# Inside the last unit of a hybrid decoder block: a later scan, output weights' low parts on both sides of it, and row 1's addition moved into the convolution

## The chip, the cores and the metric

The kernel runs on one core of one Trainium2 chip. The metric is the device time of one execution in microseconds (us); lower is better. A core has five engines that run their own instruction lists and meet only at semaphores: TensorE (PE in the rows: matrix products), VectorE (DVE), ScalarE (ACT), GpSimd (POOL), and SyncE (SP, whose queue issues all of this kernel's DMAs).

## The reference, cut to what matters

One decoder layer on x of 2048 positions by 1024 channels, float32:

```python
h = rmsnorm(x, norm_mix); proj = h @ w_in            # 4 groups of 512 channels: x_lru, g_lru, v_cm, g_cm
c = causal_depthwise_conv(x_lru, conv4_w) + conv4_b  # width 4
r, i = sigmoid(c @ gate_a + b_a), sigmoid(c @ gate_x + b_x)   # block diagonal
a = exp(-8 r softplus(-lambda));  b = sqrt(1 - a*a) * i * c
h_t = a_t * h_{t-1} + b_t                            # the scan over positions
y_lru = h * gelu(g_lru)
d = causal_depthwise_conv(v_cm * sigmoid(g_cm), dw31_w) + dw31_b   # width 31
y_cm = silu(layernorm(d))
x = x + concat(rmsnorm(y_lru), rmsnorm(y_cm)) @ w_out
x = x + (silu(rmsnorm(x) @ w_gate) * (rmsnorm(x) @ w_up)) @ w_down
out = rmsnorm(x)
```

## The kernel before, in words

Every large product is made of three float32r products: each operand is split into a high part (a cast by ACT) and a low part (operand minus high part, by POOL or DVE), and PE multiplies high by high, low by high and high by low (lines 1828 to 1830).

**Units.** The part up to the scan is done in 8 units (`UNITS`), one for each of 4 groups of 128 channels and 2 halves of 1024 positions. Unit u has two projections on PE, the short convolution, the gates, the scan of unit u (`scan(u)`, DVE) and the convolution of width 31 (`conv31(u)`, DVE): 31 instructions ("taps") on 128x1024, one after the other, each adding to `acc`. `conv31` is also the timetable of DVE: a table of places (tap numbers) says ahead of which tap other work is put. `scan(u - 1)` stands inside `conv31(u)`; the scan of the last unit, `scan(7)`, comes behind the last convolution.

**The last unit, u = 7.** PE has finished the projections and goes on as far as it may with what follows. Inside `conv31(7)` DVE also does:
- `w_out_lo(n)`, n = 0 to 3: the low parts of two chunks of the output weights each, 2 instructions. ACT makes the high parts ahead of it (`w_out_hi(n)`, line 1186). Pairs 0 and 1 lie in the two buffers `w_raw`; SP may load pair 2 only when `w_out_lo(0)` is done, and pair 3 when `w_out_lo(1)` is done (lines 466 to 469, semaphore `s_wlo`), and both loads stand in SP's queue behind the store of unit 6's y, which waits for POOL's product of the scan's result (`output(6)`, line 726).
- `norm_centre(1)`: tile 1 of 512 positions minus its mean. ACT squares the result (`squares_cm(1)`), POOL folds the squares' four chunks into one (`fold(1, "var")`, lines 789 and 791), PE makes the variance (`norm_var(1, 6)`).
- `add_row(w)` for w = 0: row tile w is 128 positions. PE multiplies y by the output weights into 4 banks of PSUM, two column halves for each of the two head groups; `add_row(w)` scales each bank by the group's rms and adds it to the residual, 4 instructions, each of which waits for its bank (`s_out[e]`). PE may write a bank again for row w + 1 only when `add_row(w)` has read it (`s_outf[e]`).

Behind `conv31(7)` DVE does `scan(7)`, `norm_scale(1)`, and for each row w: `add_row(w)` (for w > 0), a reciprocal, and `hn`, the normalised row for the FFN (line 1656).

PE's order there: gates of unit 7, `norm_mean(1)`, the products of row 0, `norm_sums_lru(1)`, `norm_var(1)`, the products of row 1, the turning of row 0's `hn` by 8 transposes (`turn_h2(0)`, line 1984), the products of row 2, `turn_h2(1)`, and so on through 16 rows. PE waits in order: what stands first holds what is behind it.

ACT's order there: `w_out_hi(0)`, `w_out_hi(1)`, the sigmoids of the gates of unit 7 (which wait for `scan(6)`, since they overwrite `uw`), `y_split(0)` (high part of row 0's y), `gate_functions(7)` (tanh, exp, one minus), and so on to `root(7)`. POOL's order: `output(6)`, the gated input, low part of y of row 0 (`y_lo`, line 820), `decay(7)` (line 757), `decay_square(7)` (line 762), `y_lo` of row 1, `scan_input(7)` (line 781), `fold(1, "var")`, `y_lo` of row 2.

After the 16 rows come the FFN's products (Strassen-like, with halves and sums) and the down projection; PE is their clock.

Of the kernel before, what the change touches and what calls it, by code (L numbers as in the profile page):

```python
# [30 lines left out]
def hybrid_block(nc, x, norm_mix, w_in, conv4_w, conv4_b, gate_a_w, gate_a_b, gate_x_w, gate_x_b,  # L31
# [14 lines left out]
    UNITS = NH * NJ  # L46
# [30 lines left out]
    with ExitStack() as ctx:  # L77
# [260 lines left out]


        SCAN_AT, CENTRE_AT, LATE_AT = 22, 16, 27  # L340
        W_OUT_AT = (12, 14, 17, 19)
        CENTRE_AT_LAST, ROW0_AT = 16, 24
        X_NORM_AT = (7, 8, 9, 10, 12, 13, 14, 15)
        X_LO_AT = (9, 10, 11, 12, 14, 15, 16, 17)
        SCAN_AT_LAST = 11
        NORM_STEP = {2: 2, 3: 5}

        TURN_FIRST = {(1, 0, 0): 0, (1, 0, 4): 1, (1, 1, 0): 2, (1, 1, 4): 3}
# [35 lines left out]
        def yb(w):  # L384

            return w % 2 + 2 * (w // TPH)
# [3 lines left out]
        def w_out_gain(k):  # L390

            return col(k % NJ, R_ONL if k < NJ else R_ONC)
# [560 lines left out]
        def _(act):  # L953
# [3 lines left out]
            def step(ins):  # L957

                steps[0] += 1
                ins.then_inc(s_act, 1)  # L960
                act.wait_ge(s_act, steps[0])
# [23 lines left out]
            def squares_lru(m):  # L985
                act.wait_ge(s_nld[m], 32)
                a.activation(ny[m][:, :, :], ny[m][:, :, :], ACT.Square).then_inc(s_sqy, 1)
# [98 lines left out]
            def gate_functions(u):  # L1086

                j = u % NJ
                act.wait_ge(s_rr, NS * (u + 1))
                if u == 0:  # L1090
                    act.wait_ge(s_rate, 3)
                a.activation(su[:, :], uw[:, :], ACT.Tanh, scale=rate[:, j:j + 1]).then_inc(s_te, 1)
                step(a.activation(uw[:, :], uw[:, :], ACT.Exp, scale=rate2[:, j:j + 1]))
                a.activation(uw[:, :], uw[:, :], ACT.Identity, bias=1.0).then_inc(s_te, 1)

            def two_minus(u):

                act.wait_ge(s_p, u + 1)
                a.activation(su[:, :], uw[:, :], ACT.Identity, scale=-1.0, bias=two[:, 0:1]).then_inc(s_two, 1)
# [79 lines left out]
            def w_out_hi(n):  # L1179

                q = PPAIRS + n
                act.wait_ge(s_w[q % 2], 32 * (q // 2 + 1))
                if n == 0:
                    act.wait_ge(s_pair[3], PPAIRS)
                for e in range(2):
                    ins = a.activation(wo_hi[:, 2 * n + e], w_raw[q % 2][:, e].rearrange("p k c -> p (k c)"),
                                       ACT.Copy, scale=w_out_gain(2 * n + e))
                ins.then_inc(s_whi, 1)

            def y_split(w):  # L1190
                act.wait_ge(s_yl[w % 2], 32 * (w // 2 + 1))
                if w >= 2:
                    act.wait_ge(s_out[3], w - 1)
                a.copy(y_hi[yb(w)][:, :, :], y_raw[yb(w)][:, :, :]).then_inc(s_yhi, 1)
# [4 lines left out]
            gates(UNITS - 1)  # L1199
            act.wait_ge(s_fin, UNITS - 1)  # L1200
            y_split(0)
            gate_functions(UNITS - 1)
            w_out_hi(2)
            two_minus(UNITS - 1)
            w_out_hi(3)
            squares_lru(1)
            y_split(1)
            squares_cm(1)
            root(UNITS - 1)
            y_split(2)  # L1210
# [210 lines left out]
        def _(dve):  # L1421
# [73 lines left out]
            def norm_centre(m, bank):  # L1495

                dve.wait_ge(s_mean, m + 1)
                v.tensor_tensor(nd[m][:, :, :], nd[m][:, :, :], ps[bank][:, None, :].broadcast_to([P, NJ, TILE]),
                                ALU.subtract).then_inc(s_dc, 1)
# [39 lines left out]
            def add_row(w, between=None):  # L1539

                if w == 4:
                    norm_rms(1)
                if w % 4 == 0:
                    dve.wait_ge(s_rms, w // 4 + 1)
                dve.wait_ge(s_xr[w % 4], 16 * (w // 4 + 1))
                line = row[w % 4]
                for group in range(2):
                    if group and between:
                        between()
                    for dh in range(2):  # L1550
                        e = 2 * group + dh
                        cols = slice(dh * TILE, (dh + 1) * TILE)
                        dve.wait_ge(s_out[e], w + 1)
                        if group:
                            dve.wait_ge(s_outf[dh], w + 1)
                        v.scalar_tensor_tensor(out=line[:, cols], in0=ps[e],
                                               scalar=rms[:, 2 * w + group:2 * w + group + 1],
                                               in1=line[:, cols], op0=ALU.mult, op1=ALU.add).then_inc(s_outf[e], 1)

            def conv31(u):  # L1560
                j = u % NJ
                t = glu[u % 2]
                last = 0
                for k in range(TAPS31):
                    place = k
                    if u == NJ - 1:

                        for g in range(TPH):
                            if place == X_NORM_AT[g]:
                                x_norm(TPH + g)  # L1570
                            if place == X_LO_AT[g]:
                                x_lo(TPH + g)
                    if place == CENTRE_AT and u == N0:
                        norm_centre(0, 6)
                    if u >= 1 and place == (SCAN_AT_LAST if u == UNITS - 1 else SCAN_AT):
                        scan(u - 1)
                    if u == UNITS - 1 and place == ROW0_AT:
                        norm_rms(0)
                        add_row(0)
                    if u == UNITS - 1 and place == CENTRE_AT_LAST:  # L1580
                        norm_centre(1, 6)
                    if u == UNITS - 1 and place in W_OUT_AT:
                        w_out_lo(W_OUT_AT.index(place))
                    if place == LATE_AT:
                        if u == N0 + 1:
                            norm_scale(0)
                    if k == 0:
                        dve.wait_ge(s_glu, (NS + 1) * (u + 1))
                        if u >= 1:
                            dve.wait_ge(s_conv31, u)  # L1590
                        ins = v.tensor_scalar(acc[:, :], t[:, 0:HALF], col(j, R_DW), col(j, R_DWB), ALU.mult, ALU.add)
                    else:
                        dve.wait_ge(s_dve, last)
                        if k == TAPS31 - 1 and u >= 2:
                            dve.wait_ge(s_dst[u % 2], 16 * (u // 2))
                        into = dst[u % 2] if k == TAPS31 - 1 else acc
                        ins = v.scalar_tensor_tensor(out=into[:, :], in0=t[:, k:k + HALF], scalar=col(j, R_DW + k),  # L1597
                                                     in1=acc[:, :], op0=ALU.mult, op1=ALU.add)
                    if k == TAPS31 - 1:
                        ins.then_inc(s_conv31, 1)  # L1600
                    else:
                        steps[0] += 1
                        last = steps[0]
                        ins.then_inc(s_dve, 1)
# [35 lines left out]
                    weight_sum(0, 0, n, 1)  # L1640

            for w in range(NT):
                if w:
                    add_row(w, first_weight_sums if w == NT - 1 else None)
                if w == 0:
                    norm_scale(1)
                if w == NT - 1:
                    a_low(0, 2)
                dve.wait_ge(s_std2, w + 1)
                step(v.reciprocal(rstd[:, w:w + 1], rstd[:, w:w + 1]))  # L1650
                if w == 0:
                    dve.wait_ge(s_gmix, 32)
                    dve.wait_ge(s_rm1, 1)
                if w >= 2:
                    dve.wait_ge(s_tr[1], w - 1)
                v.scalar_tensor_tensor(out=hn[w % 2][:, :], in0=row[w % 4][:, :], scalar=rstd[:, w:w + 1],
                                       in1=g_row[:, :], op0=ALU.mult, op1=ALU.mult).then_inc(s_hn, 1)
                for m, first in NORM_STEP.items():
                    if w - first == 0:
                        norm_centre(m, 4)  # L1660
                    if w - first == 2:
                        norm_scale(m)
                    if w - first == 4:
                        norm_rms(m)
                if w in SUM_AT:
                    for n in range(2):
                        first_half_sum(2 * SUM_AT.index(w) + n)
# [489 lines left out]
```

## Time and profile before

| | us |
|---|---|
| three timed executions | 2006.25, 2002.8, 2006.49 (median 2006.25) |
| the profiled execution, its own time | 2004.53 |
| its span in the trace | 2002.7 |
| PE busy | 1893.2 (95%) |
| POOL busy | 1249.3 (62%) |
| DVE busy | 1125.7 (56%) |
| ACT busy | 816.8 (41%) |

The span is the time from the first to the last instruction in the trace. PE is the busiest engine by far, but in the two slices of the page from 400 to 500 us, around the last unit, it is busy for seven and eight tenths, and so DVE comes level with it there (eight tenths in both).

### The profile page before, as it was taken

Reading aid. Unit: us, or ns where it says so; the run is one execution under the profiler, and the core shown is the slowest. Engines: PE = TensorE matmul, PEld = TensorE weight load, DVE = VectorE, ACT = ScalarE, POOL = GpSimd, SP = SyncE. Lnnn points to the kernel's source line nnn. Section 1 sums busy time; section 2 is a strip of 40 time slices with the busy share of each in tenths; the row PEclk is TensorE's granted clock in tenths of the full one; section 3 lists DMA queues with packets and bytes.
Section 4 is the critical chain, followed back from the end, with each engine's and each line's share of the span. In section 5 each row is a group of like instructions: output and inputs, shape, how many; then the busy total and the mean of one; then the engine's idle time right before and its main releaser. Section 6 shows DMA issues by size and latency. Waiting matters only on the chain.

```text
span 2002.7 us, 22412 instructions
## 1 busy us (share of the span) xinstructions
PE 1893.2 (95%) x8338; PEld 1554.0 (78%) x8338; DVE 1125.7 (56%) x1023; ACT 816.8 (41%) x936; POOL 1249.3 (62%) x490
## 2 busy tenths in 40 slices
PE   6999899978999799999999789999999899999997
PEld 5888687756888678878878668888888688888886
DVE  5899899988554635454454644444453123434446
ACT  6356856585553523333233433233333222322234
POOL 2477477964542567887666556766766666766663
PEclk9999999988999899999999989999999999999999
DMA  5223232245768334445234622233233565565555
GB/s 165 64 60 98 74 95 74 77 144 182 241 207 280 101 100 131 140 136 152 84 100 129 219 87 86 93 115 101 89 112 134 220 248 205 175 217 180 180 189 209
DMA packets 242335, 284.97 MB, mean 142 GB/s; under 512 B 12078, under 2 KB 167726, under 8 KB 241754
## 3 DMA queue, kind: packets, MB, share of 16 engines
q1 hardware_dynamic: 242266, 284.04, 42.9%
q8 instruction: 45, 0.74, 0.2%
q14 instruction: 24, 0.20, 0.0%
HBM read 201.68 MB, written 82.31 MB: 142 GB/s over the span
## 4 chain that ended last, share of the span: by engine, by line
PE 69%; POOL 12%; issue 7%; DVE 5%; DMA 3%; ACT 2%; SPq 1%; POOLq 0%; DVEq 0%; ACTq 0%
PE ps L1828 17%; PE ps L1829 17%; PE ps L1830 17%; PE acc L1828 6%; PE acc L1829 5%; PE acc L1830 5%; POOL b_lo L826 2%; POOL t_lo L832 2%; POOL gt L872 1%; POOL quad L881 1%; DVE acc L1597 1%; POOL fs L890 1%; DMA y_raw<-d_scr 1%; POOL f_lo L917 1%; DMA wd_raw<-in_w_down 1%
## 5 line engine op out<-in xcount | busy, mean ns | idle before, releaser
L1597 DVE SCALAR_TENSOR_TENSOR acc<-glu,par,acc 128x1024 f32<-128x1024 f32 x232 | 298.9, 1288 | 7.2
L832 POOL TENSOR_TENSOR t_lo<-t_sum,t_hi 128x2048 fp32r<-128x2048 f32 x44 | 205.0, 4658 | 135.2 <-ACT t_hi L1241 135.2
L826 POOL TENSOR_TENSOR b_lo<-m_raw,b_hi 128x1536 fp32r<-128x1536 f32 x44 | 163.9, 3724 | 164.5 <-ACT b_hi L1236 164.5
L917 POOL TENSOR_TENSOR f_lo<-f_raw,f_hi 128x2048 fp32r<-128x2048 f32 (+1 forms) x42 | 180.9, 4306 | 133.2 <-ACT f_hi L1381 133.2
L1636 DVE TENSOR_TENSOR t_sum<-m_raw 128x512 f32<-128x512 f32 x88 | 131.1, 1491 | 214.0 <-PE ps L1830 97.1
L1828 PE MATMUL ps<-h_hi,w_hi 128*128 128x512 f32 x512 | 201.9, 394 | 4.6 <-POOL w_lo L720 2.7
L1829 PE MATMUL ps<-h_lo,w_hi 128*128 128x512 f32 x512 | 200.0, 391 | 0.0
L1830 PE MATMUL ps<-h_hi,w_lo 128*128 128x512 f32 x512 | 200.0, 391 | 0.0
L1828 PE MATMUL ps<-wd_hi,f_hi 128*128 128x512 f32 x462 | 181.4, 393 | 9.9 <-POOL wd_lo L924 9.9
L1381 ACT CAST f_hi<-f_raw 128x2048 fp32r<-128x2048 f32 (+1 forms) x42 | 74.2, 1768 | 274.6 <-PE ps L1830 178.2
L1829 PE MATMUL ps<-wd_lo,f_hi 128*128 128x512 f32 x462 | 181.0, 392 | 0.0
L1830 PE MATMUL ps<-wd_hi,f_lo 128*128 128x512 f32 x462 | 180.8, 391 | 0.0
L1828 PE MATMUL ps<-a_hi,t_hi 128*128 128x512 f32 x440 | 171.4, 390 | 1.5 <-DVE p5s L1694 0.8
L1829 PE MATMUL ps<-a_lo,t_hi 128*128 128x512 f32 x440 | 171.2, 389 | 0.0
L1830 PE MATMUL ps<-a_hi,t_lo 128*128 128x512 f32 x440 | 171.2, 389 | 0.0
L1779 DVE TENSOR_TENSOR wd_raw<-wd_raw 128x1024 f32<-128x1024 f32 (+1 forms) x30 | 71.7, 2390 | 171.6 <-DMA wd_raw<-in_w_down 171.6
L1828 PE MATMUL acc<-a_hi,t_hi 128*128 128x512 f32 x264 | 106.6, 404 | 26.5 <-DVE a_lo L1612 17.0
L1828 PE MATMUL ps<-wo_hi,y_hi 128*128 128x512 f32 x256 | 107.6, 420 | 18.6 <-DVE wo_lo L1534 11.2
L1828 PEld LDWEIGHTS ps<-h_hi,w_hi 128*128 128x128 f32 x512 | 96.6, 189 | 25.2 <-POOL w_lo L720 3.2
L1636 DVE TENSOR_TENSOR t_sum<-m_raw,t_sum 128x512 f32<-128x512 f32 x88 | 112.6, 1280 | 3.0
L1830 PEld LDWEIGHTS ps<-h_hi,w_lo 128*128 128x128 f32 x512 | 96.5, 189 | 20.5
L1829 PEld LDWEIGHTS ps<-h_lo,w_hi 128*128 128x128 f32 x512 | 96.6, 189 | 19.6 <-issue 0.2
(212 smaller groups left out, 4603.0 us busy)
## 6 DMA issues: line engine op xcount, KB each, us to landing
f_raw<-f_scr SPq DMA_DIRECT2D x35, 1024.0 KB, 5.0
wd_raw<-in_w_down SPq DMA_DIRECT2D x60, 512.0 KB, 6.6
f_scr<-fs SPq DMA_DIRECT2D x110, 256.0 KB, 2.0
m_raw<-in_w_gate SPq DMA_DIRECT2D x88, 256.0 KB, 4.0
m_raw<-in_w_up SPq DMA_DIRECT2D x88, 256.0 KB, 5.0
w_raw<-in_w_in SPq DMA_DIRECT2D x32, 512.0 KB, 5.3
f_scr<-gt SPq DMA_DIRECT2D x44, 256.0 KB, 2.0
xt<-in_x SPq DMA_DIRECT2D x16, 512.0 KB, 3.7
```

The costliest lines, as they stand in the source:

```text
L826: g.tensor_tensor(b_lo[b][:, :, :, :], m_raw[b][:, 0:3], f32(b_hi[b][:, :, :, :]), ALU.subtract).then_inc(s_mlo, 1)
L832: g.tensor_tensor(t_lo[b][:, :, :, :], t_sum[b][:, :, :, :], f32(t_hi[b][:, :, :, :]), ALU.subtract).then_inc(s_mlo, 1)
L872: g.tensor_tensor(tile, tile, source[:, :], ALU.mult).then_inc(s_fm, 1)
L881: g.tensor_tensor(quad[:, into], quad[:, x1], quad[:, x2_], op).then_inc(s_qs, 1)
L917: g.tensor_tensor(f_lo[j % 3][:, 0:n], f_raw[j % 2][:, 0:n], f32(f_hi[j % 3][:, 0:n]), ALU.subtract).then_inc(s_dlo, 1)
L1381: a.copy(f_hi[j % 3][:, 0:n], f_raw[j % 2][:, 0:n]).then_inc(s_dhi, 1)
L1597: ins = v.scalar_tensor_tensor(out=into[:, :], in0=t[:, k:k + HALF], scalar=col(j, R_DW + k), in1=acc[:, :], op0=ALU.mult, op1=ALU.add)
L1636: v.tensor_tensor(into, in0, in1, ALU.subtract).then_inc(s_t, 1)
L1779: v.tensor_tensor(raw[:, 0, 0:c1 - c0], raw[:, 0, 0:c1 - c0], raw[:, 1, 0:c1 - c0], WD[m][2]).then_inc(s_t, 1)
L1828: pe.matmul(bank, lhs[0](c), rhs[0](c), start=first, stop=False, skip_group_check=more)
L1829: pe.matmul(bank, lhs[0](c), rhs[1](c), start=False, stop=False, skip_group_check=more)
L1830: mm = pe.matmul(bank, lhs[1](c), rhs[0](c), start=False, stop=last, skip_group_check=more)
```

## The change

In the last unit alone, DVE's timetable, ACT's order and the place of one addition change. `scan(6)` goes from tap 11 to tap 17; the four `w_out_lo` from taps 12, 14, 17, 19 to 16, 17, 20, 21; `norm_centre(1)` from 16 to 23; `add_row(0)` from 24 to 25; `add_row(1)`, which stood behind the convolution, gets place 29. Where places agree, the scan comes ahead of `w_out_lo`. ACT does `w_out_hi(2)` and `w_out_hi(3)` ahead of `gate_functions(7)`, and `y_split(1)` ahead of `two_minus(7)`. No instruction is added or taken away; POOL, SP and PE keep their order.

```diff
@@ -338,11 +338,11 @@
         SCAN_AT, CENTRE_AT, LATE_AT = 22, 16, 27
-        W_OUT_AT = (12, 14, 17, 19)
-        CENTRE_AT_LAST, ROW0_AT = 16, 24
+        W_OUT_AT = (16, 17, 20, 21)
+        CENTRE_AT_LAST, ROW0_AT, ROW1_AT = 23, 25, 29
...
-        SCAN_AT_LAST = 11
+        SCAN_AT_LAST = 17
@@ -1199,12 +1199,12 @@
             gates(UNITS - 1)
             act.wait_ge(s_fin, UNITS - 1)
             y_split(0)
+            w_out_hi(2)
+            w_out_hi(3)
             gate_functions(UNITS - 1)
-            w_out_hi(2)
+            y_split(1)
             two_minus(UNITS - 1)
-            w_out_hi(3)
             squares_lru(1)
-            y_split(1)
             squares_cm(1)
             root(UNITS - 1)
@@ -1579,6 +1579,8 @@
                         norm_centre(1, 6)
+                    if u == UNITS - 1 and place == ROW1_AT:
+                        add_row(1)
                     if u == UNITS - 1 and place in W_OUT_AT:
@@ -1640,7 +1642,7 @@
             for w in range(NT):
-                if w:
+                if w >= 2:
                     add_row(w, first_weight_sums if w == NT - 1 else None)
```

DVE in the last unit around the scan and the output weights, before (L1523 is the scan, L1534 `w_out_lo`, L1597 the taps, L1498 `norm_centre(1)`):

```order
L1597 SCALAR_TENSOR_TENSOR acc<-glu_168,par,acc 128x1024 x10
L1523 SCALAR_TENSOR_TENSOR cv_132<-uw,hl,su 128x1024
L1597 SCALAR_TENSOR_TENSOR acc<-glu_168,par,acc 128x1024
L1534 SCALAR_TENSOR_TENSOR wo_lo<-w_raw_140,par,wo_hi 128x1024 x2
L1597 SCALAR_TENSOR_TENSOR acc<-glu_168,par,acc 128x1024 x2
L1534 SCALAR_TENSOR_TENSOR wo_lo<-w_raw_141,par,wo_hi 128x1024 x2
L1597 SCALAR_TENSOR_TENSOR acc<-glu_168,par,acc 128x1024 x2
L1498 TENSOR_TENSOR nd_174<-nd_174,ps 128x2048
```

The same place of DVE's list with the change (two lines were added, so the taps are L1599):

```order
L1599 SCALAR_TENSOR_TENSOR acc<-glu_168,par,acc 128x1024 x15
L1534 SCALAR_TENSOR_TENSOR wo_lo<-w_raw_140,par,wo_hi 128x1024 x2
L1599 SCALAR_TENSOR_TENSOR acc<-glu_168,par,acc 128x1024
L1523 SCALAR_TENSOR_TENSOR cv_132<-uw,hl,su 128x1024
L1534 SCALAR_TENSOR_TENSOR wo_lo<-w_raw_141,par,wo_hi 128x1024 x2
L1599 SCALAR_TENSOR_TENSOR acc<-glu_168,par,acc 128x1024 x3
L1534 SCALAR_TENSOR_TENSOR wo_lo<-w_raw_140,par,wo_hi 128x1024 x2
L1599 SCALAR_TENSOR_TENSOR acc<-glu_168,par,acc 128x1024
L1534 SCALAR_TENSOR_TENSOR wo_lo<-w_raw_141,par,wo_hi 128x1024 x2
L1599 SCALAR_TENSOR_TENSOR acc<-glu_168,par,acc 128x1024 x2
L1498 TENSOR_TENSOR nd_174<-nd_174,ps 128x2048
```

Five more taps and a pair of output weights now stand ahead of the scan, and `norm_centre(1)` stands behind all four pairs.

The end of the last convolution on DVE and what follows it, before (L1556 is `add_row`, L1504 and L1506 `norm_scale(1)`, L1650 and L1656 the reciprocal and `hn`):

```order
L1556 SCALAR_TENSOR_TENSOR row_169<-ps,rms,row_169 128x512 x4
L1597 SCALAR_TENSOR_TENSOR acc<-glu_168,par,acc 128x1024 x6
L1597 SCALAR_TENSOR_TENSOR dst_149<-glu_168,par,acc 128x1024
L1523 SCALAR_TENSOR_TENSOR cv_133<-uw,hl,su 128x1024
L1504 RECIPROCAL nrs_178<-nrs_178 128x512
L1506 TENSOR_TENSOR nd_174<-nd_174,nrs_178 128x2048
L1650 RECIPROCAL rstd<-rstd 128x1
L1656 SCALAR_TENSOR_TENSOR hn_190<-row_169,rstd,g_row 128x1024
L1556 SCALAR_TENSOR_TENSOR row_170<-ps,rms,row_170 128x512 x4
```

And with the change:

```order
L1556 SCALAR_TENSOR_TENSOR row_169<-ps,rms,row_169 128x512 x4
L1599 SCALAR_TENSOR_TENSOR acc<-glu_168,par,acc 128x1024 x4
L1556 SCALAR_TENSOR_TENSOR row_170<-ps,rms,row_170 128x512 x4
L1599 SCALAR_TENSOR_TENSOR acc<-glu_168,par,acc 128x1024
L1599 SCALAR_TENSOR_TENSOR dst_149<-glu_168,par,acc 128x1024
L1523 SCALAR_TENSOR_TENSOR cv_133<-uw,hl,su 128x1024
L1504 RECIPROCAL nrs_178<-nrs_178 128x512
L1506 TENSOR_TENSOR nd_174<-nd_174,nrs_178 128x2048
L1652 RECIPROCAL rstd<-rstd 128x1
L1658 SCALAR_TENSOR_TENSOR hn_190<-row_169,rstd,g_row 128x1024
```

The four additions of row 1 (`row_170`) stood behind row 0's `hn`; now two taps, the scan, `norm_scale(1)` and row 0's `hn` stand behind them.

ACT's list from row 0's high part on (L1186 is `w_out_hi`, L1092 to L1094 `gate_functions(7)`, L1099 `two_minus(7)`, L1194 `y_split`, L987 and L991 the two squares), as a difference:

```order
 L1194 CAST y_hi_154<-y_raw_150 128x1024
-L1092 ACTIVATE su<-uw,rate 128x1024
-L1093 ACT_TABLE_LOAD
-L1093 ACTIVATE uw<-uw,rate_197 128x1024
-L1094 ACTIVATE uw<-uw 128x1024
 L1186 ACTIVATE wo_hi<-w_raw_140,par 128x1024 x2
-L1099 ACTIVATE su<-uw,two 128x1024
 L1186 ACTIVATE wo_hi<-w_raw_141,par 128x1024 x2
+L1092 ACTIVATE su<-uw,rate 128x1024
+L1093 ACT_TABLE_LOAD
+L1093 ACTIVATE uw<-uw,rate_197 128x1024
+L1094 ACTIVATE uw<-uw 128x1024
```

The gate functions now stand behind the scaling of pairs 2 and 3, which wait for their loads.

## Rows read from the trace of the kernel before

**Rows 1.** Busy times by stretch: window, its us, then each engine's busy us, PEclk.

```profile
400.00:500.00 100.00, 77.72 (x325) 61.57 (x323) 86.87 (x63) 67.14 (x74) 53.30 (x24) 0.83 0.47 162
500.00:650.00 150.00, 150.00 (x721) 123.86 (x720) 78.68 (x86) 69.26 (x100) 63.61 (x28) 1.00 0.77 242
```

**Rows 2.** Chain that ended last, 430 to 496 us: start, us, what.

```profile
432.98 4.43 DVE cv L1523
...
438.59 3.52 DVE wo_lo L1534 x2
...
493.54 0.23 PE ps L1828
```

**Rows 3.** PE in order of time: start, us, operation, [idle before <- releaser].

```profile
450.20 0.77 PE L1828 MATMUL ps<-wo_hi,y_hi 128*128 128x512 f32 x1 [3.91 <-DVE wo_lo L1534]
...
464.72 0.80 PE L1828 MATMUL ps<-wo_hi,y_hi 128*128 128x512 f32 x1 [7.33 <-DVE wo_lo L1534]
...
470.42 0.39 PE L1829 MATMUL ps<-wo_lo,y_hi 128*128 128x512 f32 x1
...
476.42 1.29 PE L1879 MATMUL ps<-nsq,mean_w 128*128 128x512 f32 x2
...
489.67 0.39 PE L1830 MATMUL ps<-wo_hi,y_lo 128*128 128x512 f32 x1
492.45 1.09 PE L1984 MATMUL ps<-ident,hn 128*128 128x128 f32 x8 [2.39 <-DVE hn L1656]
```

**Rows 4.** DVE in order of time, last unit.

```profile
412.36 13.21 DVE L1597 SCALAR_TENSOR_TENSOR acc<-glu,par,acc 128x1024 f32<-128x1024 f32 x10
432.98 4.43 DVE L1523 TENSOR_TENSOR_SCAN cv<-uw,hl,su 128x1024 f32<-128x1024 f32 x1 [7.40 <-POOL su L781]
...
452.49 2.28 DVE L1498 TENSOR_TENSOR nd<-nd,ps 128x2048 f32<-128x2048 f32 x1
...
455.88 2.47 DVE L1534 SCALAR_TENSOR_TENSOR wo_lo<-w_raw,par,wo_hi 128x1024 fp32r<-128x1024 f32 x2
...
471.30 2.73 DVE L1556 SCALAR_TENSOR_TENSOR row<-ps,rms,row 128x512 f32<-128x512 f32 x4
...
483.08 2.35 DVE L1523 TENSOR_TENSOR_SCAN cv<-uw,hl,su 128x1024 f32<-128x1024 f32 x1
...
491.11 1.28 DVE L1656 SCALAR_TENSOR_TENSOR hn<-row,rstd,g_row 128x1024 f32<-128x1024 f32 x1
```

**Rows 5.** ACT in order of time, last unit.

```profile
431.78 4.26 ACT L1186 ACTIVATE wo_hi<-w_raw,par 128x1024 fp32r<-128x1024 f32 x4
437.49 1.28 ACT L1080 ACT_TABLE_LOAD   x1 [1.45 <-DVE cv L1523]
...
444.07 1.15 ACT L1092 ACTIVATE su<-uw,rate 128x1024 f32<-128x1024 f32 x1
...
448.67 2.18 ACT L1186 ACTIVATE wo_hi<-w_raw,par 128x1024 fp32r<-128x1024 f32 x2
452.32 1.15 ACT L1099 ACTIVATE su<-uw,two 128x1024 f32<-128x1024 f32 x1 [1.47 <-POOL uw L757]
...
459.86 1.91 ACT L991 ACTIVATE nsq<-nd 128x2048 f32<-128x2048 f32 x1
...
463.08 1.06 ACT L1104 ACTIVATE su<-su 128x1024 f32<-128x1024 f32 x1
```

**Rows 6.** POOL in order of time, last unit.

```profile
432.91 2.35 POOL L810 TENSOR_TENSOR c_lo<-cv,c_hi 128x1024 fp32r<-128x1024 f32 x1
...
464.21 2.69 POOL L781 TENSOR_TENSOR su<-su,cv 128x1024 f32<-128x1024 f32 x1 [1.82 <-ACT su L1104]
...
469.31 1.28 POOL L791 TENSOR_TENSOR nsq<-nsq 128x512 f32<-128x512 f32 x1
```

**Rows 7.** DMA issues, 430 to 470 us: operation, KB each, median us to landing.

```profile
w_raw<-in_w_out SPq DMA_DIRECT2D x4, 512.0 KB, 3.9
```

**Rows 8.** SP's queue in order of time: start, us of issuing, which DMA.

```profile
442.14 8.75 SPq L468 DMA_DIRECT2D w_raw<-in_w_out  x4
```

## The prediction

> **What bounds the kernel now.** I read four views. The busy times by stretch come first: from 400 to 500 us PE is busy for 77.7 of 100 us at a mean granted clock of 0.83 of full, and from 500 to 650 us for 150.0 of 150 [rows 1]. So PE bounds the kernel on both sides of the last unit, and inside it something else does. The chain that ended last, read second, says what: from the scan at 432.98 on it runs along DVE alone (scan, output weights' low parts, taps, and so on) and goes back to PE only when row 0's `hn` has been turned, at 493.5 [rows 2]. The third view is each engine in order of time. DVE works 10 taps in 13.21 us, 1.32 each, waits 7.40 us for the scan's input, starts the scan at 432.98 and then has no gap until `hn` of row 0 ends at 492.39 (491.11 and 1.28) [rows 4]. PE waits 3.91 us before row 0's first half, 7.33 us before its second half, and 2.39 us before the turning of row 0 at 492.45 [rows 3]. From there on it has no gap for more than 150 us [rows 1, 3]. The fourth view is DMA and SP's queue [rows 7, 8]: the loads of the output weights, which the change moves.
>
> The number that decides is therefore the start of that turning, 492.45 us. PE's list behind it is unchanged and full, and everything later (stores, loads, the norms of tiles 2 and 3) hangs on rows that follow it. An earlier or later turning moves the end of the kernel by as much. What ends the wait there is DVE: PE has done row 1's products at 490.06 (489.67 and 0.39), and `hn` comes 2.3 us later [rows 3, 4].
>
> **What the change promises, if nothing waits.** DVE's work ahead of the turning loses the gap of 7.40 us and gains row 1's additions, 2.73 us as row 0's [rows 4]: 492.45 - 7.40 + 2.73 = 487.8, 4.7 us earlier. Whether it comes true depends on four instructions at tap 29, which stand ahead of two taps, `scan(7)`, `norm_scale(1)` and `hn`, and wait for PE's row 1. So I follow the chain that leads to row 1.
>
> **Step 1, the scan.** Taps 1 to 15 from 412.36 at 1.32 end at 432.2. The first pair's high parts are ready at half of 4.26 us from 431.78, at 433.9 [rows 5]. POOL runs `c_lo` until 435.26 [rows 6]. The scan beside it took 4.43 us, the one with POOL idle 2.35 [rows 4]: the first ended at 437.41, 2.15 after `c_lo`, so it stood until POOL had finished. I take the same for the pair: 435.3 + 2.4 (2.47 alone [rows 4]) = 437.7, a tap to 439.0, and the scan, alone now, ends at 441.3. That is 3.9 us later than 437.41. The Trainium skill, "SBUF — State Buffer", section "SBUF: two separate sides", says the port pair that DVE and GpSimd share is an exclusive lock, held for a whole instruction, which a DVE operation with two SBUF inputs needs. By that rule the scan costs 2.35 where POOL is idle; by the row of the scan that is moved, taken as it stands, it would cost 4.43 and the sum would be 2.1 us larger.
>
> **Step 2, gates and weights.** ACT's sigmoids wait for the scan (the 1.45 us gap ahead of the table load at 437.49 [rows 5]). The part of ACT from the scan's end to row 0's high part took until 444.07, 6.66 us, with a turn to PE and back in it; now it ends at 448.0. PE's row 0 needs `y_lo(0)`, two POOL products later: the gated input begins at some 447, 2 x 2.35, about 451.8, against 450.20 before. Its first half then runs into its second without the 7.33 us gap if pairs 2 and 3 are there, see below. POOL's `output(6)` ends at some 444.8 (2.35 as [rows 6], and 1.1 behind the DVE's next pair). SP then stores unit 6's y and issues the loads of pairs 2 and 3 together, from 445.2 on. Before, pair 2 was issued at 442.14 [rows 8]. Landing takes 3.9 us in the median [rows 7]; with a store and four transfers at once I take 450.0 for pair 2. ACT scales pair 2 and pair 3 (2.18 each [rows 5]) to 454.4. Only then come the gate functions, which took 4.60 (444.07 to 448.67 [rows 5]): 459.0, against 448.7 before. This is where the change loses 10 us on ACT and POOL.
>
> **Step 3, from the gate functions to row 1.** POOL's decay 2.4 to 461.4; two minus 1.15 [rows 5] to 462.6; two squares and the root: one square 1.9, then 4.28 from the second's start to the root's end (459.86 to 464.14 [rows 5]), to 468.8. Meanwhile DVE reaches `norm_centre(1)` at 461.0 (pair 3 cannot start before 454.4; 2.47, two taps) and ends it at 463.3 by its 2.28 [rows 4], just before the square that reads it would start at 464.5. POOL's square and `y_lo(1)` (2 x 2.35) fit before 468.8. The scan's input and the two folds took 6.38 (464.21 to 470.59 [rows 6]): 475.2. PE's variance is its next instruction and row 1 stands behind it: before, it began at 476.42 and row 1's products ended at 490.06, 13.6 us later [rows 3]. Of these 13.6, 48 products at full clock are 48 x 0.23 [rows 2] = 11.0. PE has by then been idle for about 7 us, as at 464.72, where 13 products took 5.70 us until 470.42, 0.44 each [rows 3]: that is the lower level of the granted clock, 1.2 GHz, and 2.7 us lost. 475.3 + 0.5 + 11.0 + 2.7 = 489.5. So the gap that vanishes before row 0's second half comes back before row 1, and row 1 ends at 489.5 where it ended at 490.06.
>
> **Step 4, the tail.** DVE stands before row 1's addition from about 474.0 on (ahead: `norm_centre(1)` to 463.3, two taps, row 0's addition 2.9, four taps) and is held, bank by bank, until 489.5. Then 0.7 for the last bank, two taps 2.6, and from the scan's start to the end of `hn` 9.31 (483.08 to 492.39 [rows 4]): 502.1. Queued behind the waiting addition are just these, and PE's turning of row 0 behind them; ACT's `norm_swish(1)` and with it row 1's `hn` too, at their old distance. The turning starts 9.6 us later than before.
>
> **Step 5, the clock.** PE is idle from 489.5 to 502.1, 12.6 us, where it was 2.39 before and full speed after. A gap of 7.33 us was followed by 5.7 us at half speed [rows 3]; from a gap of 12.6 us I expect the same, half of it lost. All of that would be 2.9 us, a third of it 1.0 us; I take 2.0. The Trainium skill, "TensorE: Matmul & The Clock Gate", Part 1, says the array's clock falls to half after idle time and comes back with activity; the trace agrees (0.44 after 7.33 us idle). Without a fall of the clock the sum would be 2.0 less.
>
> **The sum.** 9.6 + 2.0 = +11.6 us on the profiled execution's own 2004.53 (span 2002.7 and 1.8 around it): 2016.1. That execution lies 1.7 us under the median of 2006.25 and 1.7 over the lowest, so I leave it: 2016. A change of 0.2%, 4 us, is about what a measurement of this kernel can tell.
>
> **Edits that cost nothing here.** `norm_centre(1)` later is hidden by 1.2 us (463.3 against 464.5); without that cover each us goes on to row 1. `add_row(0)` at 25: row 0's products end near 464, DVE arrives at 466. `y_split(1)` ahead of `two_minus(7)` is free, ACT would wait for POOL's decay there.
>
> **The rivals.**
> - *The promise comes true* (faster, 2000): row 1's additions do not wait, the turning is at 487.8. It needs row 1's last bank at 474 or so; it decides at 479.5, since 479.5 + 0.7 + 2.6 + 9.31 gives the old 492.1. For it speaks that row 0's second half comes 6 us earlier. Against it: PE's variance stands ahead of row 1, and even if the old fold at 470.59 kept its time, row 1 would end at 470.7 + 0.5 + 11.0 = 482 at full clock. Chance 0.05.
> - *A draw* (2003 to 2010): the gate functions are less late than I think, because pairs 2 and 3 land at once (by 448), PE keeps its clock, and row 1 ends by 483. The turning comes within 4 us of the old one. Each of the parts has something for it, all together little. Chance 0.07.
> - *Slower, as worked out* (2009 to 2021), chance 0.80.
> - *More* (over 2021): the loads of pairs 2 and 3, now issued together behind a store, collide and land 3 us or more later; each us goes through ACT to the gate functions. Or the clock stays low through row 2. Chance 0.08.
>
> **How the numbers follow.** The low end takes row 1 and the turning at full clock (2.7 and 2.0 less) and the load 1 us earlier: +5.9, 2010.4; less the scatter of 1.7 it is 2009. The high end takes the two clock losses at their bounds (0.9 more), the scan's 2.1 and the load 1 us later, +15.6: 2020.1, and 2021 with scatter. Slower by over 0.2% is the third and fourth case and part of nothing else, 0.88; within 0.2% 0.07; faster 0.05.
>
> **What the changed profile would show.** DVE's gap of 7.40 us gone, the scan's end near 441.3 and 2.3 us long. `gate_functions(7)` starting near 454.4. No gap between the halves of row 0, a new one of 6 to 7 us before the variance, the folds ending near 475. Four additions of row 1 spread over 12 us or more with gaps that PE ends, where one piece stood. The turning of row 0 near 502 after a gap of 10 us or more, with low clock behind it. Wrong I would be if row 1's products ended before 480, or if PE's later gap (none until 650) took the delay back.

## The result, and the profile after

The change makes the kernel slower: 2016.05 us median of 4 runs (2014.15 to 2017.67) against 2004.53 of 4 runs before (2001.82 to 2006.49), ratio 1.0054, 95% interval 1.004 to 1.0068. That is 10.8 us by the ratio. The profiled execution took 2014.91 with a span of 2013.1. Since the change adds two lines, DVE's taps are L1599 and PE's products L1830 to L1832 after it.

The busy times by stretch, changed kernel, beside [rows 1]:

```profile
400.00:500.00 100.00, 69.28 (x289) 54.55 (x287) 79.54 (x59) 58.57 (x63) 48.18 (x22) 0.81 0.37 129
500.00:510.00 10.00, 6.46 (x22) 5.47 (x23) 3.45 (x3) 7.82 (x10) 2.84 (x2) 0.56 0.94 312
510.00:660.00 150.00, 150.00 (x722) 123.98 (x721) 75.58 (x85) 66.84 (x100) 64.56 (x29) 1.00 0.77 238
```

Both engines did less in the same 100 us: PE 69.3 us for 77.7, DVE 79.5 for 86.9. PE's stretch without a gap begins 10 us later, and the 10 us ahead of it run at a granted clock of 0.56.

DVE in order of time, changed kernel (start, us, operation, [idle before <- releaser]), beside [rows 4]:

```profile
434.51 3.56 DVE L1534 SCALAR_TENSOR_TENSOR wo_lo<-w_raw,par,wo_hi 128x1024 fp32r<-128x1024 f32 x2 [1.79 <-ACT wo_hi L1186]
...
439.19 2.34 DVE L1523 TENSOR_TENSOR_SCAN cv<-uw,hl,su 128x1024 f32<-128x1024 f32 x1
...
453.59 2.48 DVE L1534 SCALAR_TENSOR_TENSOR wo_lo<-w_raw,par,wo_hi 128x1024 fp32r<-128x1024 f32 x2 [3.73 <-ACT wo_hi L1186]
...
469.68 5.26 DVE L1599 SCALAR_TENSOR_TENSOR acc<-glu,par,acc 128x1024 f32<-128x1024 f32 x4
482.91 0.75 DVE L1556 SCALAR_TENSOR_TENSOR row<-ps,rms,row 128x512 f32<-128x512 f32 x1 [7.98 <-PE ps L1832]
485.56 0.75 DVE L1556 SCALAR_TENSOR_TENSOR row<-ps,rms,row 128x512 f32<-128x512 f32 x1 [1.90 <-PE ps L1832]
488.28 0.75 DVE L1556 SCALAR_TENSOR_TENSOR row<-ps,rms,row 128x512 f32<-128x512 f32 x1 [1.97 <-PE ps L1832]
491.00 0.75 DVE L1556 SCALAR_TENSOR_TENSOR row<-ps,rms,row 128x512 f32<-128x512 f32 x1 [1.97 <-PE ps L1832]
...
494.18 2.35 DVE L1523 TENSOR_TENSOR_SCAN cv<-uw,hl,su 128x1024 f32<-128x1024 f32 x1
...
502.20 1.28 DVE L1658 SCALAR_TENSOR_TENSOR hn<-row,rstd,g_row 128x1024 f32<-128x1024 f32 x1
```

The gap of 7.40 us ahead of the scan is gone, and row 1's addition, tap 29, waits four times for PE, 13.8 us together (7.98, 1.90, 1.97, 1.97). The scan of unit 7, `norm_scale(1)` and row 0's `hn` stand behind it.

PE in order of time, changed kernel, beside [rows 3]:

```profile
452.35 0.47 PE L1830 MATMUL ps<-wo_hi,y_hi 128*128 128x512 f32 x1 [1.84 <-POOL y_lo L820]
...
459.71 0.50 PE L1830 MATMUL ps<-wo_hi,y_hi 128*128 128x512 f32 x1 [1.68 <-DVE wo_lo L1534]
...
476.61 2.04 PE L1881 MATMUL ps<-nsq,mean_w 128*128 128x512 f32 x2 [4.67 <-POOL nsq L791]
...
503.55 1.97 PE L1986 MATMUL ps<-ident,hn 128*128 128x128 f32 x8 [12.58 <-DVE hn L1658]
505.17 0.78 PE L1830 MATMUL ps<-wo_hi,y_hi 128*128 128x512 f32 x1
...
509.02 0.40 PE L1830 MATMUL ps<-wo_hi,y_hi 128*128 128x512 f32 x1
```

The gap of 7.33 us between the halves of row 0 has shrunk to 1.68. Ahead of the variance there is one of 4.67 that was not there, and ahead of the turning one of 12.58 where 2.39 stood. The 8 transposes behind it take 1.97 us where they took 1.09, and 9 products lie between 505.17 and 509.02, 0.43 each; the granted clock from 503.5 to 509.0 is 0.51, the lower level of 1.2 GHz.

ACT, changed kernel, beside [rows 5], and below it POOL, beside [rows 6]:

```profile
441.61 1.28 ACT L1080 ACT_TABLE_LOAD   x1 [5.05 <-DVE cv L1523]
...
451.37 2.19 ACT L1186 ACTIVATE wo_hi<-w_raw,par 128x1024 fp32r<-128x1024 f32 x2 [3.07 <-DMA w_raw<-in_w_out]
453.96 2.19 ACT L1186 ACTIVATE wo_hi<-w_raw,par 128x1024 fp32r<-128x1024 f32 x2 [0.40 <-DMA w_raw<-in_w_out]
456.06 1.14 ACT L1092 ACTIVATE su<-uw,rate 128x1024 f32<-128x1024 f32 x1
```

```profile
433.43 2.37 POOL L810 TENSOR_TENSOR c_lo<-cv,c_hi 128x1024 fp32r<-128x1024 f32 x1
...
475.20 1.26 POOL L791 TENSOR_TENSOR nsq<-nsq 128x512 f32<-128x512 f32 x1
```

The gate functions start at 456.1 for 444.1, and the folds end at 476.5 for 470.6. SP's queue and the DMA view, changed kernel, beside [rows 7, 8]:

```profile
445.33 2.24 SPq L468 DMA_DIRECT2D w_raw<-in_w_out  x4
```

```profile
w_raw<-in_w_out SPq DMA_DIRECT2D x4, 512.0 KB, 5.8
```

The four transfers go out in 2.24 us where they took 8.75, and land in 5.8 us in the median for 3.9.

**Where the time went.** What `c_lo` on POOL waits for is the same in all kernels of this study, and yet it starts at 432.91 before and at 433.43 after, so I count from there. The turning of row 0 comes 59.5 us behind it before and 70.1 after: +10.6. DVE's own list accounts for nearly all of it: 13.8 of waiting in row 1's addition and 2.7 for the addition, 1.8 and 3.7 of new gaps before two pairs of weights, less the old gap of 7.4, less 4.5 that scan and weights together take less beside POOL (15.4 us for 19.9); that makes 10.2. Row 1's products themselves end at 490.96 for 490.06, 0.4 us later counted from `c_lo`: PE delivers them when it did, and what is new is how much of DVE's list stands behind them.

### The profile page after: what moved, and what is told of

Same layout as the page of the kernel before. It is cut to its first block, busy times and chain, and to the rows that moved or that the text cites. A ratio compares the mean times of both kernels' runs of the same rounds, so it can differ in the third digit from the quotient of the medians.

```text
span 2013.1 us, 22412 instructions
## 1 busy us (share of the span) xinstructions
PE 1891.8 (94%) x8338; PEld 1554.2 (77%) x8338; DVE 1122.5 (56%) x1023; ACT 816.7 (41%) x936; POOL 1249.1 (62%) x490
## 4 chain that ended last, share of the span: by engine, by line
PE 70%; POOL 13%; issue 7%; ACT 3%; DMA 3%; DVE 3%; SPq 1%; POOLq 0%; DVEq 0%; ACTq 0%
PE ps L1830 17%; PE ps L1831 17%; PE ps L1832 17%; PE acc L1830 6%; PE acc L1831 5%; PE acc L1832 5%; POOL b_lo L826 2%; POOL t_lo L832 2%; POOL gt L872 1%; POOL quad L881 1%; POOL fs L890 1%; POOL f_lo L917 1%; DVE t_sum L1638 1%; PE ps L1855 1%; POOL w_lo L720 1%
## 5 line engine op out<-in xcount | busy, mean ns | idle before, releaser
L1599 DVE SCALAR_TENSOR_TENSOR acc<-glu,par,acc 128x1024 f32<-128x1024 f32 x232 | 299.0, 1289 | 7.2
L1830 PE MATMUL ps<-h_hi,w_hi 128*128 128x512 f32 x512 | 202.4, 395 | 4.5 <-POOL w_lo L720 2.6
L1832 PE MATMUL ps<-h_hi,w_lo 128*128 128x512 f32 x512 | 200.3, 391 | 0.0
L1830 PE MATMUL ps<-wd_hi,f_hi 128*128 128x512 f32 x462 | 182.1, 394 | 10.2 <-POOL wd_lo L924 10.2
L1832 PE MATMUL ps<-wd_hi,f_lo 128*128 128x512 f32 x462 | 181.4, 393 | 0.0
L1830 PE MATMUL ps<-a_hi,t_hi 128*128 128x512 f32 x440 | 171.6, 390 | 1.5 <-DVE p5s L1696 0.8
L1832 PE MATMUL ps<-a_hi,t_lo 128*128 128x512 f32 x440 | 171.3, 389 | 0.0
L1830 PE MATMUL acc<-a_hi,t_hi 128*128 128x512 f32 x264 | 106.2, 402 | 25.6 <-DVE a_lo L1614 17.0
L1830 PE MATMUL ps<-wo_hi,y_hi 128*128 128x512 f32 x256 | 106.2, 415 | 11.0 <-POOL y_lo L820 9.4
L1830 PEld LDWEIGHTS ps<-h_hi,w_hi 128*128 128x128 f32 x512 | 96.9, 189 | 25.0 <-POOL w_lo L720 3.0
L1832 PEld LDWEIGHTS ps<-h_hi,w_lo 128*128 128x128 f32 x512 | 96.6, 189 | 20.3
```

The lines of the kernel that those rows point to most:

```text
L1830: pe.matmul(bank, lhs[0](c), rhs[0](c), start=first, stop=False, skip_group_check=more)
L1832: mm = pe.matmul(bank, lhs[1](c), rhs[0](c), start=False, stop=last, skip_group_check=more)
```

## The experiments

Theory A is the prediction's: row 1's addition in the convolution holds DVE for PE's row 1, which stands behind a variance that has become late. Theory B: the late scan and the late gate functions cost by themselves, wherever row 1's addition stands.

**1. Row 1's addition back behind the convolution, the rest of the change kept.**

```diff
-                    if u == UNITS - 1 and place == ROW1_AT:
-                        add_row(1)
...
-                if w >= 2:
+                if w:
                     add_row(w, first_weight_sums if w == NT - 1 else None)
```

> The changed kernel with one part undone: row 1's addition stands behind the last convolution again; scan at tap 17, output weights' low parts, norm_centre(1) at 23 and ACT's order as changed. Theory A (the loss is row 1's addition at tap 29, which holds VectorE for TensorE's row 1): the turning of row 0 comes 13 us earlier than in the changed kernel (near 490 us in the trace, VectorE without a gap behind the second pair of output weights), and the kernel is some 4 us faster than before: ratio about 0.998, 2000.5 against 2004.5. Theory B (the loss is the late scan, which makes gates, gate functions and folds late, wherever row 1's addition stands): most of the loss stays, ratio 1.004 to 1.006, turning near 502.

Measured: ratio to before 0.9983 (0.9974 to 0.9993), 3.4 us faster. PE, this kernel:

```profile
477.34 2.05 PE L1879 MATMUL ps<-nsq,mean_w 128*128 128x512 f32 x2 [6.50 <-POOL nsq L791]
...
490.89 1.03 PE L1984 MATMUL ps<-ident,hn 128*128 128x128 f32 x8
```

DVE has row 0's `hn` ready at 488.6, 4.4 us earlier than before counted from `c_lo` (433.54 here). The turning has no gap ahead of it: now PE's row 1, which runs until the turning starts, sets it, and of the 4.4 us 2.2 arrive. Theory B falls: with the scan and the gate functions as late as in the changed kernel (`gate_functions(7)` at 456.8), the loss is not there.

**2. Row 1's addition at tap 29 alone, in the kernel before.**

```diff
+                    if u == UNITS - 1 and place == ROW1_AT:
+                        add_row(1)
...
-                if w:
+                if w >= 2:
                     add_row(w, first_weight_sums if w == NT - 1 else None)
```

> The kernel before with one part of the change alone: row 1's addition at tap 29. Theory A: row 1's products end where they did, near 489 to 490 us, VectorE stands before row 1's addition for some 11 us in pieces, the turning of row 0 comes at 502, and the kernel is 9 to 11 us slower than before, ratio about 1.005, as much as the whole change. Theory B: row 1's addition there costs no more than its own 2.7 us ahead of hn, ratio at most 1.0015.

Measured: ratio 1.0054 (1.0041 to 1.0067), the whole loss of the change. DVE and, below it, PE of this kernel:

```profile
482.18 0.75 DVE L1556 SCALAR_TENSOR_TENSOR row<-ps,rms,row 128x512 f32<-128x512 f32 x1 [1.49 <-PE ps L1832]
484.83 0.75 DVE L1556 SCALAR_TENSOR_TENSOR row<-ps,rms,row 128x512 f32<-128x512 f32 x1 [1.90 <-PE ps L1832]
487.55 0.75 DVE L1556 SCALAR_TENSOR_TENSOR row<-ps,rms,row 128x512 f32<-128x512 f32 x1 [1.97 <-PE ps L1832]
490.27 0.75 DVE L1556 SCALAR_TENSOR_TENSOR row<-ps,rms,row 128x512 f32<-128x512 f32 x1 [1.97 <-PE ps L1832]
```

```profile
502.81 1.97 PE L1986 MATMUL ps<-ident,hn 128*128 128x128 f32 x8 [12.59 <-DVE hn L1658]
```

It waits 7.3 us, not the 11 I expected: DVE is there at 480.7, where in the changed kernel it is there at 474.9. The 7.3 and the 2.7 of the addition make 10.0 of the 10.2 us by which the turning is later from `c_lo` on (433.05 here). The wait need not be long to cost: with the addition ahead of `hn`, the turning starts 12.6 us behind row 1's products in this kernel and in the changed one (12.59 and 12.58), whatever else DVE saves. Nor does it need a late variance, for PE's variance has no gap ahead of it here, as before.

**3. The changed kernel, the sums of tile 1's squares behind row 1's products on PE.**

```diff
-                if w == 0:
+                if w == 1:
                     free_aux(1, AUX_USES)
                     norm_sums_lru(1, 7)
                     pe.wait_ge(s_dc, 2)
                     norm_var(1, 6)
```

> The changed kernel, and on TensorE the sums of tile 1's squares (norm_sums_lru(1), norm_var(1)) stand behind row 1's products, ahead of the turning of row 0, where they stood ahead of row 1's products. Theory A in its second half (what makes row 1 late is the variance ahead of it, which waits for the folds): row 1's products start near 467 to 469 us, when y_lo(1) is there, and end near 480; VectorE waits 5 us instead of 17 in row 1's addition; the turning comes at 493 to 494, as before the change: ratio 1.000 to 1.001. If instead row 1's low part of y or the clock sets row 1's start, the turning stays at 500 or later and the ratio at 1.004 or more.

Measured: ratio 1.0016 (1.0005 to 1.0026), 3.2 us slower than before, 7.6 faster than the changed kernel. PE, this kernel:

```profile
470.37 0.50 PE L1830 MATMUL ps<-wo_hi,y_hi 128*128 128x512 f32 x1 [2.37 <-POOL y_lo L820]
...
487.60 2.05 PE L1881 MATMUL ps<-nsq,mean_w 128*128 128x512 f32 x2
...
497.54 1.97 PE L1986 MATMUL ps<-ident,hn 128*128 128x128 f32 x8 [7.89 <-DVE hn L1658]
```

Row 1's products start at 470.4 instead of near 478, and most of the loss goes: with the addition at tap 29, the variance ahead of row 1 is worth these 7.6 us. By the ratio that is 1 to 3 us short of what I expected, and the turning is at 497.5 for 493 to 494. Two reasons show in the rows: row 1 waits for its own low part of y until 470.4 (I had 467 to 469), and the variance, now at 487.6 to 489.6, comes too late for `norm_scale(1)`: from the scan's start to the reciprocal of row 0 there are 9.65 us (486.36 to 496.01), 7.84 before.

**4. The changed kernel with ACT's old order.**

```diff
+            gate_functions(UNITS - 1)
             w_out_hi(2)
+            two_minus(UNITS - 1)
             w_out_hi(3)
-            gate_functions(UNITS - 1)
-            y_split(1)
-            two_minus(UNITS - 1)
             squares_lru(1)
+            y_split(1)
             squares_cm(1)
```

> The changed kernel with ScalarE's old order (gate functions ahead of the scaling of pairs 2 and 3). By my reckoning pair 3 comes some 6 us later, so row 0's second half waits again, norm_centre(1) and with it squares and folds come 2.5 us later, and the turning of row 0 comes near 504 to 506, 2 to 3 us later than in the changed kernel: ratio to before 1.006 to 1.007. The rival (the late gate functions are what costs) expects a gain: turning 5 us or more earlier than in the changed kernel, ratio 1.003 or less.

Measured: ratio 1.0066 (1.0053 to 1.0079), by the two ratios 2.4 us slower than the changed kernel, where I expected it, though the two intervals overlap. PE's row 0 waits again between its halves in this kernel:

```profile
462.09 0.80 PE L1830 MATMUL ps<-wo_hi,y_hi 128*128 128x512 f32 x1 [4.15 <-DVE wo_lo L1534]
```

The rival expected a gain, and there is none, although the gate functions start 8 us earlier here (448.1 for 456.1): `squares_cm(1)` then waits 5.5 us for `norm_centre(1)`, which stands behind the late pair 3, and the folds end at 477.2, no earlier. From `c_lo` on (433.33) the turning comes 0.5 us later than in the changed kernel, less than the 2 to 3 I expected.

**5. ACT's new order alone, in the kernel before.**

```diff
+            w_out_hi(2)
+            w_out_hi(3)
             gate_functions(UNITS - 1)
-            w_out_hi(2)
+            y_split(1)
             two_minus(UNITS - 1)
-            w_out_hi(3)
             squares_lru(1)
-            y_split(1)
```

> The kernel before with one part of the change alone: ScalarE's order (pairs 2 and 3 scaled ahead of the gate functions, row 1's high part ahead of two_minus). Pair 3 can be loaded only when the low part of pair 1 is done, near 450 us, so ScalarE stands for it with the gate functions behind it: they start near 457 instead of 444, the folds end near 478 instead of 470.6, row 1's products start 1.5 to 2 us later. By theory A the turning comes 1 to 2 us later, ratio 1.0005 to 1.001. If the late gate functions were a cost by themselves (theory B), 8 us of delay would show: ratio 1.003 or more.

Measured: ratio 0.9993 (0.9984 to 1.0002), no difference that can be told, and below the 1.0005 to 1.001 I expected. ACT and PE of this kernel:

```profile
456.73 2.19 ACT L1186 ACTIVATE wo_hi<-w_raw,par 128x1024 fp32r<-128x1024 f32 x2 [6.03 <-DMA w_raw<-in_w_out]
458.83 1.14 ACT L1092 ACTIVATE su<-uw,rate 128x1024 f32<-128x1024 f32 x1
```

```profile
494.57 1.03 PE L1984 MATMUL ps<-ident,hn 128*128 128x128 f32 x8
```

Counted from `c_lo` (434.44 here), the gate functions start 13.2 us later than before, and the turning 0.6 us. So theory B fails a second time. The late chain is not wholly hidden: the folds end 8.1 us later and row 1's products 3.0, `hn` is ready at 492.5, and the turning starts 2.1 us behind it, without a gap, when row 1 is done. But before, `hn` came 2.3 us behind row 1's products, and that covers most of the 3.0.

**6. The scan at tap 15 in the kernel before.**

```diff
-        SCAN_AT_LAST = 11
+        SCAN_AT_LAST = 15
```

> The kernel before with the scan of unit 6 at tap 15 instead of 11, behind the pairs 0 and 1 of the output weights; row 1's addition behind the convolution. VectorE's gap of 7.4 us goes, but gates, unit 6's y, and the loads of pairs 2 and 3 that stand in the queue behind its store, all come some 8 us later, and VectorE then waits for pair 2. By my reckoning the turning of row 0 comes 4 to 5 us later than before, ratio 1.002 to 1.0025. A reader of the timetable alone expects VectorE's gap to be gained: ratio 0.997.

Measured: ratio 1.0012 (1.0003 to 1.0022), 2.4 us slower. SP's queue and DVE of this kernel:

```profile
452.34 2.24 SPq L468 DMA_DIRECT2D w_raw<-in_w_out  x4
```

```profile
437.59 3.56 DVE L1534 SCALAR_TENSOR_TENSOR wo_lo<-w_raw,par,wo_hi 128x1024 fp32r<-128x1024 f32 x2 [11.44 <-ACT wo_hi L1186]
...
458.21 2.29 DVE L1498 TENSOR_TENSOR nd<-nd,ps 128x2048 f32<-128x2048 f32 x1 [7.52 <-PE ps L1879]
...
462.99 2.63 DVE L1534 SCALAR_TENSOR_TENSOR wo_lo<-w_raw,par,wo_hi 128x1024 fp32r<-128x1024 f32 x2 [1.29 <-ACT wo_hi L1186]
```

The direction is as reckoned; the size is half, 2.4 us by the ratio and 2.3 at the turning for the 4 to 5 expected. And the old gap is not gone, as I had thought: pair 0, at tap 12, waits for its high parts, 11.44 us, of which 3.6 are `c_lo`'s later start in this execution (436.52). Two more come, 7.52 before `norm_centre(1)`, for which PE's mean is late behind the gates, and 1.29 before pair 2; the loads go out 6.6 us later, counted from `c_lo`. Of these gaps 6.4 us come back, since the scan and the four pairs take 13.5 us, beside less of POOL, where they took 19.9. The scan's place by itself gains nothing; experiment 1 gains, where the weights' places, `norm_centre(1)` and ACT's order move with it. Which of these it takes was not tried one by one.

**7. Experiment 1, and in SP's queue pair 2's load ahead of the store of unit 6's y.**

```diff
                     store_d(u - 1)
+                    if u == UNITS - 1:
+                        load_raw(PPAIRS + 2)
                     store_y(u - 1)
...
-            load_raw(PPAIRS + 2)
             load_raw(PPAIRS + 3)
```

> The changed kernel with row 1's addition behind the convolution again (as in the first experiment), and in SP's queue the load of pair 2 stands ahead of the store of unit 6's y instead of behind it. If the loads that stand behind that store are what makes the gate functions and the folds late (step 2 of the prediction), the load is issued near 438.5 instead of 445.3, ScalarE scales pair 2 without a wait, the gate functions start near 453 instead of 457, folds end near 473.5 instead of 477.2, and the turning comes 3 to 4 us earlier than in the first experiment: ratio to before 0.996 to 0.997. If the landing of the loads does not matter, it stays at 0.998.

Measured: ratio 0.9973 (0.9963 to 0.9984), 5.4 us faster than before. ACT and PE of this kernel (one line more, so L1187 and L1093):

```profile
450.81 2.18 ACT L1187 ACTIVATE wo_hi<-w_raw,par 128x1024 fp32r<-128x1024 f32 x2
453.94 2.20 ACT L1187 ACTIVATE wo_hi<-w_raw,par 128x1024 fp32r<-128x1024 f32 x2 [0.95 <-DMA w_raw<-in_w_out]
456.05 1.13 ACT L1093 ACTIVATE su<-uw,rate 128x1024 f32<-128x1024 f32 x1
```

```profile
476.60 2.05 PE L1880 MATMUL ps<-nsq,mean_w 128*128 128x512 f32 x2 [4.28 <-POOL nsq L792]
...
490.16 1.03 PE L1985 MATMUL ps<-ident,hn 128*128 128x128 f32 x8
```

`c_lo` starts at 436.06 here, 2.5 us later than in experiment 1, so the rows read later than they are: from there the gate functions start after 20.0 us for 23.2, the folds end after 40.4 for 43.7, and the turning comes after 54.1 for 57.4. The loads go out 4.7 us behind `c_lo` instead of 11.9, the gate functions gain 3.2 us of it, and these 3.2 us go through to the turning, as step 2 of the prediction had it. Against experiment 1 the two ratios differ by 0.0010 with intervals that overlap; the traces, not the times, show it.

**8. Experiment 7, and on PE the sums of squares between the two halves of row 1.**

```diff
                 for group in range(2):
                     if group:
                         norm_steps(w)
+                    if group and w == 1:
+                        free_aux(1, AUX_USES)
+                        norm_sums_lru(1, 7)
+                        pe.wait_ge(s_dc, 2)
+                        norm_var(1, 6)
```

> As the run before it, and on TensorE the sums of tile 1's squares stand between the two halves of row 1's products. Row 1's first half then starts at about 466 to 468 instead of behind the variance, row 1 ends near 480, and VectorE alone sets the turning (hn of row 0 near 485). If TensorE's row 1 was still the later of the two, this gains 1 to 3 us more, ratio 0.995 to 0.996; if the gap of some 5 us that TensorE then has before the turning lowers its clock, the gain is taken back and the ratio is that of the run before.

Measured: ratio 0.9967 (0.9955 to 0.9979), 6.6 us faster than before, less than the 0.995 to 0.996 expected. It is the lowest ratio here, with an interval that overlaps experiment 7's. PE, this kernel:

```profile
466.87 0.50 PE L1829 MATMUL ps<-wo_hi,y_hi 128*128 128x512 f32 x1 [2.81 <-POOL y_lo L821]
...
486.85 1.09 PE L1985 MATMUL ps<-ident,hn 128*128 128x128 f32 x8 [1.09 <-DVE hn L1657]
```

Counted from `c_lo` (433.75), row 1 starts 8.5 us earlier than in experiment 7, and the turning waits 1.09 us for `hn`: DVE sets it again. It comes after 53.1 us, 1.0 less than in experiment 7; DVE itself waits 1.08 us in `norm_scale(1)` for the variance, which is later now.

| kernel | `c_lo` starts | turning of row 0 starts | between | against before | ratio to before |
|---|---|---|---|---|---|
| before | 432.91 | 492.45 | 59.5 | | 1 |
| the change | 433.43 | 503.55 | 70.1 | +10.6 | 1.0054 |
| 1, row 1's addition back | 433.54 | 490.89 | 57.4 | -2.2 | 0.9983 |
| 2, row 1's addition alone | 433.05 | 502.81 | 69.8 | +10.2 | 1.0054 |
| 3, variance behind row 1 | 433.57 | 497.54 | 64.0 | +4.4 | 1.0016 |
| 4, ACT's old order | 433.33 | 503.95 | 70.6 | +11.1 | 1.0066 |
| 5, ACT's order alone | 434.44 | 494.57 | 60.1 | +0.6 | 0.9993 |
| 6, scan at 15 alone | 436.52 | 498.31 | 61.8 | +2.3 | 1.0012 |
| 7, load earlier | 436.06 | 490.16 | 54.1 | -5.4 | 0.9973 |
| 8, and variance in between | 433.75 | 486.85 | 53.1 | -6.4 | 0.9967 |

## Why the prediction was right

The prediction said 2016 us, and 2016.05 was measured. The agreement to a tenth is luck; the steps are not. The change lost where and how the prediction said, and two of its terms were too small.

- *What decides is the start of row 0's turning.* Right: in the nine kernels the ratio follows it within about 2 us (the table), though each place comes from one trace and each ratio from 4 to 12 executions.
- *Step 1.* The scan would end at 441.3, alone and 2.35 us long; it ended at 441.5 after 2.34. That it is longer only beside a POOL product was read from two rows, and held. Experiment 1 has a third: `scan(7)` starts at 478.12, a POOL product ends at 479.50, and the scan takes 3.53 us, so it ends 2.15 us behind the product, as the prediction's row did. The Trainium skill's lock ("SBUF — State Buffer", "SBUF: two separate sides") gives the same, and by the other reading the sum would have been 2.1 us too large.
- *Step 2.* Pair 2 was to be there at 450.0, the gate functions at 454.4; they were at 451.4 and 456.1. The term was mis-sized: with store and loads together the four landings took 5.8 us in the median, where the prediction has 4.8 from the issue to pair 2. Experiment 7 showed that this term goes through to the turning.
- *Step 3.* The folds were to end at 475.2 and did at 476.5, row 1's products at 489.5 and did at 491.0: the 1.5 us of step 2, carried. Experiment 3 showed the mechanism, the variance ahead of row 1. `norm_centre(1)` was reckoned at 461.0 and came at 462.1; the 461.0 comes by way of pair 2, while the terms in the step's brackets, pair 3 from 454.4 on, give 459.5. One reading in the step was incomplete: the 2.7 us of low clock were put down to PE standing idle, and PE stood for 4.67 us, not 7, since the 32 products of one column ahead of the variance took 5.57 us. The first products of row 1 ran at the lower level in the kernel before too, with no gap ahead of them, behind 32 such products (472.93 to 476.42). Its clock over these first products:

```profile
477.00:480.50 3.50, 3.50 (x10) 2.44 (x9) 3.43 (x3) 2.70 (x5) 0.00 (x0) 0.53 0.00 0
```

So most of the 2.7 was in the old 13.6 us from the variance to row 1's end already: it is 14.4 now, 0.7 more.
- *Step 4.* DVE was to stand there from 474.0 on (474.9), and 12.6 us to pass from row 1's end to the turning (12.58). Experiments 1 and 2 showed that this step alone is the loss: taken out, the rest of the change gains; put in alone, it costs the whole.
- *Step 5.* 2.0 us for the clock. The tenth product behind the turning starts 5.47 us after the turning's start, 3.01 before: 2.5 us. But the table's ratios follow the turning without it, so the times of the whole kernel don't show this term by itself.
- *The sum.* Two terms were short and something behind them made up for it. By the trace's own clock the turning came 11.1 us later (9.6 in the prediction), and with the 2.5 that makes 13.6, not 11.6. PE's next gap stands ahead of the last row's products, and up to there the 13.6 us are whole. PE before, and below it after:

```profile
662.81 0.80 PE L1828 MATMUL ps<-wo_hi,y_hi 128*128 128x512 f32 x1 [7.36 <-POOL y_lo L820]
...
683.62 0.47 PE L1828 MATMUL ps<-a_hi,t_hi 128*128 128x512 f32 x1 [0.71 <-DVE a_lo L1612]
```

```profile
676.41 0.79 PE L1830 MATMUL ps<-wo_hi,y_hi 128*128 128x512 f32 x1 [7.52 <-POOL y_lo L820]
...
696.06 0.47 PE L1830 MATMUL ps<-a_hi,t_hi 128*128 128x512 f32 x1 [0.71 <-DVE a_lo L1614]
```

At the FFN's first product that waits for `a_lo` (the second row of each) 12.4 are left, and from there to the end of the span it took 1317.0 us for 1319.1, so that the span grew by 10.4. The instructions of these stretches are the same, and the ten traces give 1313.4 to 1320.7 us for the second: these 2.0 us are within what scatters from one execution to the next. That the total fell on the prediction is the luck in it.
- *The promise of 4.7 us.* As a rival it failed, but the filled gap was real: with the addition outside, DVE's `hn` came 4.4 us earlier in experiment 1. "Its work fits on DVE" was right and not enough. With the addition inside, `hn` hangs on PE's row 1, and even with it outside PE's row 1 was the new limit.

## What to carry to other kernels

Before work is moved ahead of a chain on an in-order engine, ask when its input comes, not whether the engine has room: four additions of 0.7 us each put 12.6 us of tail behind another engine's products. A filled gap is a gain only as far as the next limit allows, so read both sides of a wait: here DVE's 4.4 us became 2.2 until PE's variance and one load's place in the queue were moved too. A load that stands in a queue behind a store waits for the store's producer; that place was worth 3 us, and no engine's list shows it.

## What the runs showed that I had not expected

- What leads up to `c_lo` is the same in all these kernels, and it still starts at anything from 432.9 to 436.5 us (the table's first column). A trace must be read from a mark behind that scatter.
- The FFN's part scatters as well. From its first product that waits for `a_lo` to the end of the span it took 1319.1 us before (683.62 to 2002.7) and 1313.4 in experiment 6 (689.86 to 2003.3), with the same instructions. One part of it is a wait of 1.2 us at a time, which comes in some iterations and not in others. PE's waits behind 520 us, kernel before, and below it those of experiment 6:

```profile
PE acc L1828 <- DVE gt L1678: 5.1, 5, 1.2
```

```profile
PE acc L1828 <- DVE gt L1678: 0.2, 1, 0.2
```

That is why a profile of one execution can show 6 us more at the turning and a span only 0.6 us longer, and why the ratios of many runs, not the spans, stand in the table.
